# Two of the 48 low parts of each expert pass formed by GpSimd instead of VectorE

## The reference, cut to what matters

```python
def moe_swiglu(h, router_w, wg, wu, wd):
    tokens = h.reshape(b * s, d)
    probs = jax.nn.softmax((tokens @ router_w).astype(jnp.float32), axis=-1)
    top_p, top_i = lax.top_k(probs, TOP_K)
    ...
    for e in range(N_EXPERTS):
        y = y + gates[:, e:e + 1] * swiglu(tokens, wg[e], wu[e], wd[e])

def swiglu(h, wg, wu, wd):
    return (jax.nn.silu(h @ wg) * (h @ wu)) @ wd
```

## Time and profile before

| | |
|---|---|
| median of three runs | 2266.33 us (2265.36 to 2267.01) |
| the profiled execution's own time | 2267.55 us |
| its span in the trace | 2265.8 us |
| PE busy | 2223.3 us, 98% |
| DVE busy | 1565.7 us, 69% |
| ACT busy | 1237.9 us, 55% |
| POOL busy | 375.3 us, 17% |

### The profile page before, as it was taken

One profiled execution on the slowest core, in us unless ns is written; L12 is line 12 of the kernel. 1 busy time (PEld: TensorE's weight loads), 2 busy tenths in 40 slices (PEclk: granted clock), 3 DMA queues, 4 the chain that ended last, 5 costly groups with the idle time before them and its releaser, 6 DMA issues.

```text
span 2265.8 us, 29186 instructions
## 1 busy us (share of the span) xinstructions
PE 2223.3 (98%) x10255; PEld 1826.5 (81%) x10255; DVE 1565.7 (69%) x1725; ACT 1237.9 (55%) x1524; POOL 375.3 (17%) x180
## 2 busy tenths in 40 slices
PE   7999999999999999999999999999999999999997
PEld 6888888888888888888877888888877888888875
DVE  4466686666655666665564466686679999999998
ACT  5445454454444444444435445454457887878875
POOL 1111211222222222222222111221220000000000
PEclk9999999999999999999999999999999999999999
DMA  7454545555555555555655464545589999999996
GB/s 246 149 191 158 185 153 189 182 175 191 184 193 195 185 191 195 188 184 189 200 167 168 149 197 152 186 158 196 194 311 342 360 367 366 365 381 366 367 362 224
DMA packets 264461, 515.40 MB, mean 227 GB/s; under 512 B 15528, under 2 KB 19740, under 8 KB 263324
## 3 DMA queue, kind: packets, MB, share of 16 engines
q1 hardware_dynamic: 260880, 502.51, 64.8%
q0 software_dynamic: 3312, 11.90, 1.7%
q10 hardware_dynamic: 200, 0.05, 0.0%
HBM read 508.81 MB, written 13.65 MB: 231 GB/s over the span
## 4 chain that ended last, share of the span: by engine, by line
PE 78%; DVE 10%; issue 5%; ACT 4%; DMA 3%; ACTq 0%; DVEq 0%; POOLq 0%; SPq 0%
PE acc L1565 20%; PE acc L1567 20%; PE acc L1566 20%; PE acc L1859 4%; PE acc L1861 4%; PE acc L1860 4%; DVE w_lo L982 3%; DMA scr<-tokens_dram,slot_token 3%; ACT w_hi L643 2%; PE X L1840 1%; PE X L1673 1%; DVE sm L987 1%; DVE nat L1125 1%; PE X L1593 0%; DVE eg L1469 0%
## 5 line engine op out<-in xcount | busy, mean ns | idle before, releaser
L643 ACT ACTIVATE w_hi<-raw 128x1024 fp32r<-128x1024 f32 x744 | 778.6, 1058 | 608.6 <-PE acc L1567 558.0
L982 DVE TENSOR_TENSOR w_lo<-raw,w_hi 128x1024 fp32r<-128x1024 f32 x606 | 758.4, 1271 | 477.3 <-ACT w_hi L643 474.9
L1565 PE MATMUL acc<-w_hi,a_hi 128*128 128x512 f32 x1632 | 643.7, 394 | 4.0 <-DVE w_lo L982 2.4
L1567 PE MATMUL acc<-w_hi,a_lo 128*128 128x512 f32 x1632 | 636.4, 390 | 0.0
L1566 PE MATMUL acc<-w_lo,a_hi 128*128 128x512 f32 x1632 | 635.8, 390 | 0.0
L576 POOL TENSOR_TENSOR w_lo<-raw,w_hi 128x1024 fp32r<-128x1024 f32 x138 | 337.8, 2448 | 1304.9 <-ACT w_hi L643 1005.3
L1565 PEld LDWEIGHTS acc<-w_hi,a_hi 128*128 128x128 f32 x1632 | 306.8, 188 | 67.7 <-DVE w_lo L982 3.8
L1567 PEld LDWEIGHTS acc<-w_hi,a_lo 128*128 128x128 f32 x1632 | 306.4, 188 | 64.9
L1566 PEld LDWEIGHTS acc<-w_lo,a_hi 128*128 128x128 f32 x1632 | 306.9, 188 | 61.3
L1859 PE MATMUL acc<-w_hi,a_hi 128*128 128x512 f32 x752 | 302.4, 402 | 4.2 <-DVE w_lo L982 4.1
L1861 PE MATMUL acc<-w_hi,a_lo 128*128 128x512 f32 x752 | 294.1, 391 | 0.0
(11 more groups left out here) (236 smaller groups left out, 1492.4 us busy)
## 6 DMA issues: line engine op xcount, KB each, us to landing
raw<-in_w_in SPq DMA_DIRECT2D x112, 1024.0 KB, 5.0
raw<-in_moe_w_gate SPq DMA_DIRECT2D x64, 1024.0 KB, 12.9
more_raw<-in_moe_w_up SPq DMA_DIRECT2D x64, 1024.0 KB, 12.7
raw<-in_dense_w_gate SPq DMA_DIRECT2D x44, 1024.0 KB, 5.2
raw<-in_dense_w_up SPq DMA_DIRECT2D x44, 1024.0 KB, 5.1
raw<-in_dense_w_down SPq DMA_DIRECT2D x44, 1024.0 KB, 5.1
raw<-in_w_out SPq DMA_DIRECT2D x32, 1024.0 KB, 5.2
raw<-in_moe_w_down SPq DMA_DIRECT2D x32, 1024.0 KB, 12.3
```

The lines of the kernel that those rows point to most:

```text
L643: nc.scalar.activation(w_hi[:, slot], raw_tile(tile)[1][:, u % TILE_UNITS], ACT.Copy)\
L982: nc.vector.tensor_tensor(w_lo[:, slot], raw_tile(u // TILE_UNITS)[1][:, u % TILE_UNITS], w_hi[:, slot].bitcast(F32), ALU.subtract).then_i ...
L1565: nc.tensor.matmul(dst, hi, w_hi[:, slot, c], start=first and c == 0, stop=False)
L1567: ins = nc.tensor.matmul(dst, lo, w_hi[:, slot, c], start=False, stop=last and c == UNIT_CHUNKS - 1)
```

## The change

POOL forms the low parts of the units 15 and 31 of every pass, the last unit of each up job. `POOL_PASS` holds the two numbers; `pools(u)` says whose a unit is; `low_ready` counts 46 of DVE's and 2 of POOL's per pass; `split_lo` on DVE returns without an instruction for POOL's units. In POOL's loop over the passes two calls of `low_parts` stand ahead of the gather and the addition, and two more behind the loop for the last pass.

```diff
+    POOL_PASS = (2 * UP_UNITS - 1, 4 * UP_UNITS - 1)
...
         def pools(u):
-            return u < M0 and u % 4 == POOL_UNIT
+            return u % 4 == POOL_UNIT if u < M0 else (u - M0) % PASS_UNITS in POOL_PASS
...
         def low_ready(eng, u, per=0, i=None):
             if u >= M0:
-                eng.wait_ge(lo_ready, lin(3 * M0 // 4 + u - M0 + 1, per, i))
+                n, v = divmod(u - M0, PASS_UNITS)
+                by_pool = len([p for p in POOL_PASS if p <= v])
+                if pools(u):
+                    eng.wait_ge(pool_ready, lin(M0 // 4 + n * len(POOL_PASS) + by_pool, len(POOL_PASS) * per // PASS_UNITS, i))
+                else:
+                    eng.wait_ge(lo_ready, lin(3 * M0 // 4 + n * (PASS_UNITS - len(POOL_PASS)) + v + 1 - by_pool,
+                                              (PASS_UNITS - len(POOL_PASS)) * per // PASS_UNITS, i))
...
                 low_ready(pool, u - 1, per, i)
                 nc.gpsimd.tensor_tensor(w_lo[:, u % SPLIT_SLOTS],
-                                        raw[:, (u // TILE_UNITS) % RAW_SLOTS, u % TILE_UNITS],
+                                        raw_tile(u // TILE_UNITS)[1][:, u % TILE_UNITS],
                                         w_hi[:, u % SPLIT_SLOTS].bitcast(F32), ALU.subtract).then_inc(pool_ready, 1)
...
             with pool.Fori(0, passes - 1) as i:
+                for u in POOL_PASS:
+                    low_parts(M0 + u, PASS_UNITS, i)
                 gather_rows(1, 1, i)
                 add_rows(i)
+            for u in POOL_PASS:
+                low_parts(M0 + u, PASS_UNITS, passes - 1)
```

## The result

The changed kernel takes 2279.49 us at the median of four runs (2278.89 to 2279.74), against 2266.18 us for the kernel before in the same comparison: 13.3 us more, a ratio of 1.0059 with a 95% interval of 1.0045 to 1.0073. It is slower, and clear of the noise, within the predicted range and 4.7 us under the predicted 2284.2.

A forecast was written before the change was run, and what follows sets the result against it. PE was taken as the bound, with DVE close behind and PE's waits hanging on DVE's silu stretch. 16 x 1.12 = 17.9 us added to the 2266.33 us median gave 2284.2 us, range 2274 to 2291.

The forecast's parts named there:

- What bounds a pass: PE bounds at 69.86 of 70.55 us; its waits at unit 16 and for gathered rows hang on DVE's silu stretch.
- The meeting of the two engines: At the silu steps, POOL's low part goes between L1465 and L1469, about 2.8 us; L1469 is held throughout; chance 0.70.
- The rows of L1164: Earlier meeting: POOL's low part took 2.82 us and held the second L1164, both operands in SBUF, until its end.
- The three rivals that turned on the order or the length of the hold: At the silu steps: DVE first, 2276.5 us (0.11); POOL first, 2289.4 (0.07); half a hold, about 2266.3 (0.05).
- the one without a hold: At the silu steps, POOL hinders nobody and lighter DVE gains 6.7 us: 2259.6 us, chance 0.07.
- First half: Units 15 and 16: unit 15's lateness is hidden by the longer wait behind it; unit 16 starts 1.12 us later.
- Second half: L1469 ends 1.11 us later, unit 32 loses 0.7, and PE is 1.12 later in all after the gather.
- lets it go 1.12 later, and PE, which already waited for it, is 1.12 later in all at L1840: Behind unit 40: L1396 releases the gather 1.12 us later, and PE, waiting for its rows, loses the same.
- the 72.8 that was named as a sign: Sign that the forecast is right: a whole pass takes 72.8 us instead of 70.55.
- 17.9: Predicted total loss in us over all passes: 16 places, two per pass, at 1.12 us each.
- The first rival: POOL hinders nobody: 3.2 us gained at nine unit 16 or 32 places, 3.5 at seven gathers; 2259.6 us, chance 0.07.

The follow-up runs named there:

- e5: Kernel before, one idle 128x960 subtraction put on VectorE ahead of the second silu step, nothing new on POOL: 2280.82 us, ratio 1.0065.
- e3: Changed kernel with the second operand of both silu steps in PSUM instead of SBUF: 2263.93 us, ratio 0.9997 to the kernel before.
- e7: Kernel before, later pass loads bringing three of four row blocks of each down tile (outputs wrong): 2260.53 us, ratio 0.9979.
- e1: Changed kernel with only unit 15 of each pass given to POOL: 2271.2 us, ratio 1.0032 to the kernel before.
- e2: Changed kernel with only unit 31 of each pass given to POOL: 2272.05 us, ratio 1.0031 to the kernel before.
- e6: Changed kernel, second silu operand in PSUM, down tiles loading three of four row blocks (outputs wrong): 2256.11 us, ratio 0.9960 to the kernel before.

## Why the prediction was right, and which term was too large

**What bounds a pass.** Right: the change acted through the stretch of DVE from the first silu step to the low part of unit 16 or 32, and e5, which delays that stretch by other means, gives the loss again.

**The meeting of the two engines.** Right, in order and size. POOL's low part comes behind L1465 and ahead of L1469, 2.77 us where 2.80 was worked out; L1469 is held to the end. The rows of L1164 were the right neighbours to read it from. e3 shows the cause: take one operand of the silu steps out of SBUF, and POOL's work beside them costs nothing. The three rivals that turned on the order or the length of the hold, and the one without a hold, are excluded by sixteen second steps of 2.758 to 2.774 us.

**First half.** Right: unit 15 at 0.52 (0.54 predicted) and hidden, unit 16 at 1.07 (1.12 predicted).

**Second half.** Unit 32 was right with 0.64 against 0.7. The step that failed in size is "lets it go 1.12 later, and PE, which already waited for it, is 1.12 later in all at L1840". The token numbers did come about 1.06 later (1878.70, less 2.63, against 1875.01 in the earlier trace rows). But the rows landed sooner (7.2 us in this pass and 6.5 at the median, instead of 8.3), so they were there when PE came, and PE was only 0.55 later. I had taken the landing time of the gather as fixed, when it depends on what else is being loaded. With the measured terms the sum is 8 x 1.07 + 7 x 0.55 + 1.07 = 13.5, against 13.3 measured, and a pass comes out 1.62 longer; the passes from the second gather on were 1.45 to 1.67 longer, 72.2 us and not the 72.8 that was named as a sign. The 4.4 us between 17.9 and 13.5 are 7 x 0.57 = 4.0 for this term and 0.4 for nine places at 1.07 instead of 1.12. That the sum meets the medians within 0.2 is in part luck: its terms come from one pass, and the two profiled executions lie only 11.3 us apart (spans of 2277.1 and 2265.8). One reason is the first gather, for which PE waited 1.93 us before and 0.33 after.

That the load queue beside it bears on the gather is shown by e7. But the two don't go in step. In e1 and e2 the weight loads landed in 8 to 9 us instead of 12 to 13, and the rows still took 8.1 and 8.0; in e3 the gate loads issued about a gather (from 5 us ahead of its start to 9 us behind it) landed in up to 15.3 us at the median, and the rows took 8.2. To 6.4 or 6.5 us the rows came down only where the gate loads about the gather landed in under 7, as in the last four gathers of the changed kernel (6.1 to 6.8). That there it was the longer pass that emptied the queue is a reading, not tried by itself. It agrees with the rows' landing from pass to pass, 7.9, 7.7, 7.2, then 6.4 to 6.5, and with e5, where they went from 8.5 to 6.8 without any load moved by POOL.

**What was not foreseen.** The first rival had the kernel gain 6.7 us if nothing hindered DVE. e3 removed the hindrance and gained nothing that can be measured, because the loads follow so closely: at 69.5 us a pass they fall behind until, after four passes, ACT waits for them. With lighter loads the same relief is worth 4.4 us (e7 to e6). So in the kernel before TensorE and the loads are both within some 2% of being the bound (a pass takes 70.55 us there, 69.4 in e6 with lighter loads, and 71.4 to 72.0 at the end of e3, where the loads hold it up), and lightening VectorE alone, as e3 does, did not make it faster by anything that can be measured. No version was found that beats the kernel before with all its work done; e3 is level with it.

## What to carry to other kernels

Before a piece of VectorE's work goes to GpSimd, look at what VectorE does next to it: here an instruction with two operands in SBUF stood still until GpSimd's was done, 2.77 us instead of 0.69, and the loan cost more than it brought; with one operand in PSUM it took 0.69 again. Two operands in SBUF are not the only case: in attention a 128x8 `tensor_scalar` with one tensor read from SBUF (L987) took 2.33 us beside POOL's low part (at 1390.15 in the kernel before), where the 128x8 `tensor_scalar` of L994 took 0.17 with POOL idle. Read the price from the places where the two already meet in the trace, and don't take a recorded start for the start of the work. And don't carry a transfer's landing time over unchanged: here the gathered rows went from 8.3 to 6.5 us in the slower kernel, and in e3, whose first passes were faster, the loads became the bound after four of them.

## What the runs showed of the hardware that was not expected

The loads gave way only after four passes of e3. In its first three passes and most of the fourth they still landed in 11 to 13 us at the median (1700 to 2000 us); from 2010 us on in 14 to 16. For some 280 us this kernel lived on loads that came ahead, so a look at one early pass would have shown a gain that the whole run does not have.
